# One phase in place of five at the end of each second-block layer: gates, MLA attention, head norms, branch products and output projection

## What is computed

```python
for i in range(DEPTH):                                  # DEPTH = 2
    u = rms_norm(h, norm_mix_g[i])
    z = u @ w_in[i]
    z_rwkv, z_mla, z_gdn, z_gate = split_cols_2(z, ...)
    o_a, v_first = rwkv7_branch(...)                    # ends in a per-head norm, a bonus and a gate
    o_b = mla_branch(...)                               # 8 heads, keys of 96, causal softmax
    o_c = gdn_branch(...)                               # ends in a per-head norm and a gate
    g_a, g_b, g_c = split(sigmoid(z_gate), 3)           # each 256 x 1024
    merged = g_a * (o_a @ w_br_rwkv[i]) + g_b * (o_b @ w_br_mla[i]) + g_c * (o_c @ w_br_gdn[i])
    h = h + merged @ w_out[i]
    u2 = rms_norm(h, norm_ffn_g[i])                     # then an FFN (layer 0) or a mixture of experts (layer 1)
```

## Time and profile before

| | us |
|---|---|
| median of 3 runs | 4079.12 (4063.91, 4079.12, 4082.13) |
| the profiled execution's own time | 4070.22 |
| its span | 4068.4 |
| TensorE busy | 3807.3 |
| VectorE, ScalarE, GpSimd busy | 727.7, 576.2, 155.3 |
| mean granted TensorE clock | 0.94 of 2.4 GHz |

### The profile page before, as it was taken

One profiled execution on the slowest core, in us unless ns is written; L12 is line 12 of the kernel. 1 busy time (PEld: TensorE's weight loads), 2 busy tenths in 40 slices (PEclk: granted clock), 3 DMA queues, 4 the chain that ended last, 5 costly groups with the idle time before them and its releaser, 6 DMA issues. The chain is left out here.

```text
span 4068.4 us, 45964 instructions
## 1 busy us (share of the span) xinstructions
PE 3807.3 (94%) x19340; PEld 2809.7 (69%) x19340; DVE 727.7 (18%) x1642; ACT 576.2 (14%) x1320; POOL 155.3 (4%) x107
## 2 busy tenths in 40 slices
PE   8998999999999988799999987969999999999999
PEld 6766677775676767546767676438787787787786
DVE  1023201004201354311013553120000000000001
ACT  1013201002201331101003312010010111010101
POOL 0000000000000021000101210010000000000000
PEclk9997999999999987699999976979999999999999
DMA  6321233333232400234324001418787787777863
GB/s 273 147 91 73 93 155 155 150 127 138 99 155 101 153 10 1 81 152 173 155 104 163 10 1 68 165 61 311 262 297 262 261 297 261 275 285 261 298 261 142
DMA packets 57336, 664.27 MB, mean 163 GB/s; under 512 B 7904, under 2 KB 8544, under 8 KB 11392
## 3 DMA queue, kind: packets, MB, share of 16 engines
q1 hardware_dynamic: 52272, 649.91, 42.1%
q10 hardware_dynamic: 4944, 12.65, 0.8%
HBM read 661.49 MB, written 1.05 MB: 163 GB/s over the span
## 5 line engine op out<-in xcount | busy, mean ns | idle before, releaser
L3237 PEld LDWEIGHTS psum<-arena,ring 128*128 128x128 f32 x7168 | 833.8, 191 | 111.7 <-issue 109.8
L3237 PE MATMUL psum<-arena,ring 128*128 128x128 f32 x7168 | 836.0, 274 | 8.2 <-DVE arena L3291 7.2
L613 PE MATMUL psum<-xT_norm,ring 128*128 128x256 f32 x3520 | 771.0, 380 | 0.0
L613 PEld LDWEIGHTS psum<-xT_norm,ring 128*128 128x128 f32 x3520 | 670.3, 191 | 112.7 <-issue 23.9
L3244 PE MATMUL psum<-ring,arena 128*128 128x512 f32 x896 | 420.3, 593 | 0.0
L624 PE MATMUL psum<-ring,arena 128*128 128x512 f32 x880 | 386.6, 592 | 0.0
L624 PEld LDWEIGHTS psum<-ring,arena 128*128 128x128 f32 x880 | 167.2, 190 | 187.0 <-issue 184.2
L3296 DVE TENSOR_TENSOR arena<-arena,psum 128x128 f32<-128x128 f32 x224 | 65.0, 290 | 1100.9 <-ACT arena L3275 1100.9
L672 DVE TENSOR_TENSOR arena<-arena,psum 128x256 f32<-128x256 f32 x110 | 46.4, 421 | 1061.9 <-ACT arena L653 1061.9
L3244 PEld LDWEIGHTS psum<-ring,arena 128*128 128x128 f32 x896 | 153.6, 191 | 110.9 <-issue 110.9
L3275 ACT ACTIVATE arena<-psum 128x128 f32<-128x128 f32 x224 | 62.5, 279 | 1140.0 <-PE psum L3237 1140.0
(11 more groups left out here) (496 smaller groups left out, 2899.9 us busy)
## 6 DMA issues: line engine op xcount, KB each, us to landing
ring<-in_moe_w SPq DMA_DIRECT2D x224, 1536.0 KB, 6.7
ring<-in_ffn_w SPq DMA_DIRECT2D x50, 3072.0 KB, 10.1
ring<-in_feat_w SPq DMA_DIRECT2D x12, 2048.0 KB, 8.5
ring<-in_merge_w SPq DMA_DIRECT2D x12, 2048.0 KB, 8.2
ring<-in_ffn_w SPq DMA_DIRECT2D x15, 1024.0 KB, 10.0
ring<-in_merge_w SPq DMA_DIRECT2D x12, 1024.0 KB, 7.2
ring<-in_ev_in_w SPq DMA_DIRECT2D x4, 2048.0 KB, 7.8
ring<-in_od_in_w SPq DMA_DIRECT2D x4, 2048.0 KB, 7.8
```

The costliest lines, as they stand in the source:

```text
L613: last = pe.matmul(prog.psum[:, t, m * S:(m + 1) * S], wm[:, k, t * P:(t + 1) * P], prog.xT[:, k, :], start=(k == 0), stop=(k == KT - 1))
L3237: last = pe.matmul(psum[:, s % 2, x * P:(x + 1) * P], m[:, x, i, :], xg[:, i, :], start=(i == 0), stop=(i == KT - 1))
```

## The change

Both layers' five phases become one, `join_branches`. What it does:

- The merge weights are packed anew into 11 pieces of 2 MB: six gate pieces, three branch pieces (both column halves of one branch), two projection pieces (four of the eight row blocks, all 1024 columns). The bytes are the same 22 MB per layer.
- Piece 0 is started on SP inside `chains`, once `r_made` has reached the first block's RWKV output; pieces 1 to 3 at the head of the new phase, the others as their ring places come free.
- TensorE's order is written out: the gate tiles stand between the steps of the attention and are kept in SBUF (12 tiles of 128 x 512); then the mixers' transposes, the other gates, the branch products, and the projection, whose first half of rows (`project(0)`) runs ahead of the transposes of the second half of the merged tile.
- The head norms run on VectorE, ScalarE and GpSimd in the same phase, between the attention's steps. Gate tiles use PSUM banks 5 to 7, branch products 4 and 5, scores 0 and 1, transposes 2 and 3, the projection 0 to 3.
- The three weight pieces of layer 0's feed-forward are started on SP after the branch products of MLA's second half.

```diff
 def chains(prog, layer, kept, o, merge_weights):
+        @ph.block.sync
+        def _(sp):
+            sp.wait_ge(r_made, R_MADE["y0"])
+            merge_weights.start(sp, 0)
...
-def finish_branches(prog, layer, kept, o, mem):
-def mla_attention(prog, kept, o):
-def merge(prog, weights, w_out, oT, merged):
+def join_branches(prog, layer, kept, o, weights, next_weights):
...
+        @ph.block.sync
+        def _(sp):
+            for i in (1, 2, 3):
+                weights.start(sp, i)
+            for n in range(5):
+                sp.wait_ge(gate_sum, TB * (n + 1))
+                weights.start(sp, 4 + n)
+            sp.wait_ge(gate_sum, TB * 6)
+            weights.start(sp, 9)
+            sp.wait_ge(branch_sum, 8)
+            weights.start(sp, 10)
+            if next_weights:
+                sp.wait_ge(branch_sum, 10)
+                for i in range(3):
+                    next_weights.start(sp, i)
...
+            def project(j):
+                weights.wait(pe, 9 + j)
+                for n, (b, c) in enumerate(columns):
...
+                    for k in range(4):
+                        if n == 0 and k % 2 == 0:
+                            pe.wait_ge(mT_copied[k // 2], j + 1)
+                        last = pe.matmul(psum[:, n, :], mT[:, 4 * j + k, b * P:(b + 1) * P], w[:, k, c * BANK:(c + 1) * BANK],
+                                         start=(j == 0 and k == 0), stop=(j == 1 and k == 3), skip_group_check=True)
...
+            score(0)
+            gate(0)
+            turn(0)
+            score(1)
+            gate(1)
+            values(0)
+            turn(1)
+            score(2)
+            gate(2)
+            values(1)
+            turn(2)
+            gate(3)
+            values(2)
+            gate(4)
+            gate(5)
+            turn_branch(0)
+            gate(6)
+            turn_branch(1)
+            gate(7)
+            turn_branch(2)
+            for n in range(8, 12):
+                gate(n)
+            for n in range(6):
+                branch(n)
+            branch(6)
+            branch(7)
+            turn_merged(0)
+            for n in range(8, 12):
+                branch(n)
+            project(0)
+            turn_merged(1)
+            project(1)
...
+            act.activation(squares[:, 1], by_head(g_y), ACT.Square).then_inc(head_squared, 1)
+            exponentials(0)
+            squash(0)
+            copy_turned(0)
+            act.wait_ge(centred, 1)
+            act.activation(squares[:, 0], by_head(r_y), ACT.Square).then_inc(head_squared, 1)
+            exponentials(1)
+            squash(1)
+            copy_turned(1)
+            exponentials(2)
+            squash(2)
+            copy_turned(2)
+            act.wait_ge(head_mean, 2)
+            act.activation(stat, stat, ACT.Sqrt).then_inc(head_rooted, 1)
+            squash(3)
...
             chains(prog, i, kept, o, mer)
-            mer.prefetch(0, 1, 2, 3)
-            finish_branches(prog, i, kept, o, mem)
-            mla_attention(prog, kept, o)
-            transposes(prog, [o[:, b, k * P:(k + 1) * P] for k in range(12) for b in range(TB)], oT.rearrange("p a b -> p (a b)"))
-            merge(prog, mer, out_w, oT, (merged, mem.at))
-            if i == 0:
-                ffn[4].prefetch(0, 1, 2)
-            add_projection(prog, out_w, merged, mT, mem.take(2, BANK))
+            join_branches(prog, i, kept, o, mer, ffn[4] if i == 0 else None)
```

More of the change, by code:

```diff
@@ L1601, with chains @@
 QUADS = 8
-def chains(prog, layer, kept, o):
+def chains(prog, layer, kept, o, merge_weights):
     r, g, psum = kept.r, kept.g, prog.psum
@@ L2924, in take, with __init__ @@
         return v.rearrange(f"p ({' '.join(names)}) -> p {' '.join(names)}", **kw)
-def finish_branches(prog, layer, kept, o, mem):
-    r, g = kept.r, kept.g
-    squares, bonus_v = mem.take(2, TB, NH8, HD), mem.take(TB, NH8, HD)
+class MergeWeights(Weights):
+    def __init__(self, prog, layer):
+        flat, pieces, at = prog.inp[f"merge_w{layer}"], [], 0
+        for place in (0, 1, 2, 3, 0, 1, 2, 3, 0, 1, 2):
+            n = P * KT * BANK
+            pieces.append((flat[at:at + n].rearrange("(p c) -> p c", p=P), place * KT * BANK))
+            at += n
+        super().__init__(prog, pieces)
@@ new lines, in join_branches @@
+def join_branches(prog, layer, kept, o, weights, next_weights):
+    r, g, psum, ident = kept.r, kept.g, prog.psum, prog.ident
+    early = Arena(prog, kept.free_at)
+    squares, bonus_v = early.take(2, TB, NH8, HD), early.take(TB, NH8, HD)
+    kept.load_rows(prog, layer, early)
+    oT = Arena(prog, kept.free_at).take(3, PAIRS, S)
+    t_sb, pT_sb = (Arena(prog, kept.kept_at).take(2, 2, 2 * BANK)[:, i] for i in range(2))
+    state_at = kept.qT_at - 2 * PAIRS * HD
+    least, total = Arena(prog, state_at).take(2, 3, 8)[:, 0], Arena(prog, state_at).take(2, 3, 8)[:, 1]
+    gates_a, gates_b = Arena(prog, kept.g_at).take(8, BANK), Arena(prog, kept.r_tok_at + TB * BANK).take(4, BANK)
+    gates = [gates_a[:, n] if n < 8 else gates_b[:, n - 8] for n in range(12)]
+    mT = Arena(prog, kept.qT_at).take(KT, S)
+    junk = Arena(prog, kept.kT_at).take(2, BANK)
@@ new lines, in join_branches @@
+    first = prog.const_at["zero"][0]
+    attended = ((0, 0, 4), (1, 0, 2), (1, 2, 2))
+    members = [[[x * 4 + at + j for j in range(n)] for x in range(2)] for b, at, n in attended]
+    keys = lambda i: (attended[i][0] + 1) * P
+    hidden_keys = lambda i: prog.consts[:, first + P - attended[i][0] * P:first + S]
+    probs_of = lambda i: t_sb[:, i % 2].rearrange("p (m n) -> p m n", n=keys(i))
+    value_bank, gate_bank = psum[:, 4, :], lambda n: psum[:, 5 + n % 3, :]
+    tiles = [(j, x, b) for j in range(2) for x in range(3) for b in range(TB)]
@@ new lines, in _ @@
+            exponentials(1)
[7 more added lines that the diff above has]
+            squash(3)
+            squash(4)
+            squash(5)
+            copy_branch(0)
+            squash(6)
+            copy_branch(1)
+            squash(7)
+            copy_branch(2)
+            for n in range(8, 12):
+                squash(n)
@@ new lines, in _ @@
+            for n in range(3):
+                copy_branch(n)
+            for n in range(8):
+                weigh(n)
+            copy_merged(0)
+            for n in range(8, 12):
+                weigh(n)
+            copy_merged(1)
+            for n, (b, c) in enumerate(columns):
+                dve.wait_ge(bank_full, n + 1)
+                at = prog.x[:, b, c * BANK:(c + 1) * BANK]
+                dve.tensor_tensor(at, psum[:, n, :], at, ALU.add).then_inc(tail.added, 1)
+            tail.on_vector(dve)
@@ L3434, in second_weights @@
     tok = chunk_weights(prog, prog.inp[f"tok_w{layer}"], TOK_CHUNKS, (4096, 14336))
-    flat, pieces, at = prog.inp[f"merge_w{layer}"], [], 0
-    for i in range(12):
-        n = P * (KT if i % 2 == 0 else 4) * BANK
-        pieces.append((flat[at:at + n].rearrange("(p c) -> p c", p=P), i % 4 * 4096))
-        at += n
-    return feat, tok, Weights(prog, pieces)
+    return feat, tok, MergeWeights(prog, layer)
 def build(nc, inp, tables, out):
```

341 lines of the change are left out of this document (231 added, 110 removed).

## The result

The changed kernel takes 4006.52 us (median of four executions, 4002.36 to 4018.45); the kernel before, run beside it on the same chip, 4077.36 (4063.91 to 4082.13). The ratio is 0.9836, 95% interval 0.9804 to 0.9869. The forecast was 4010, with 3993 to 4034 as its range.

What follows compares the result with a forecast made beforehand. TensorE, busy 94% of the span, was taken as the bound, with about 52 and 50 us of slack in the two layers. Phases of 176.4 us gain 33.9 and 31.0, together 64.9; from 4074.7 that gives 4010, range 3993 to 4034.

Steps and rivals of the forecast that it cites:

- The joined phase: Merged phase of each layer: 169.7 us of TensorE work plus entry, clock, waits and tail, 176.4 us in all.
- Margins: Hand-overs from VectorE and ScalarE in the attention: each group's probabilities ready 2 to 4 us before TensorE needs them.
- GpSimd's slowing: VectorE runs slower where GpSimd works on the same tiles; margins take most of it, 0.5 us added.
- Table loads: ScalarE's alternating exponentials and sigmoids: about nine loads a layer, 1.28 us each, no cost to TensorE if margins hold.
- The norms cost nothing, because gates cover them: Head norms in the merged phase: hidden behind gates; without that cover they would cost their 18 us again.
- Weights: Merge-weight loads, with piece 0 started 48 us ahead of the phase: all at zero; a late piece costs 8.8 to 18.6.
- other phases moving by more than a few us: Stated sign of a wrong prediction, beside a merged phase of over 190 us.
- A: Rival: attention hand-overs through VectorE and ScalarE still make TensorE wait, 6.3 + 6.5 us, about 4023; chance 0.10.
- B: Rival: clock falls between the gates, three falls a layer at about 2.8 us, 17 in all, 4027; chance 0.11.
- C: Rival: piece 0 lands late and gate 0 waits 5 to 15 us a layer, 4020 to 4040; chance 0.03.
- D: Rival: gates run at the low clock, 6.9 us more per tile, up to 165 us more, 4175; chance 0.02.
- The baseline: Starting point of the forecast: 4074.7 us, the middle of four executions from 4063.9 to 4082.1, 9 either way.

Runs made afterwards that it cites:

- e6: Changed kernel with five ScalarE copies of 128x1024 ahead of each group's exponentials, holding them back; 4040.90 us, 0.9914 of the kernel before.
- e3: Changed kernel with all attention steps first on TensorE, the first six gates after them, and ScalarE's first four sigmoids behind its square root; 4051.70 us.
- e1: Changed kernel with piece 0 of the merge weights started at the head of the joined phase instead of inside `chains`; 4021.01 us, 0.9876 of the kernel before.

## Why the prediction was right, and where not

- **The joined phase: right.** 176.4 us a layer were worked out, 175.0 and 174.6 measured. TensorE is busy for 171.8 and the other 3.2 are the entry (0.4), the copy ahead of `project(1)` (0.34 against 0.5) and the tail (2.51 against 2.5). The clock was up 6.0 us after the end of `chains` in layer 0 and 5.1 in layer 1, which is 5.6 and 4.7 after TensorE's first product (5.2 to 6.4 assumed); against full speed the scores and gate 0 lose some 3 us (3.75 for 16 records that were put at 1.7, 8.06 for a tile of 6.9), where the sum has 2.8. The transposes were put too high: eight in 0.87 us are 7.0 for 64, not 7.7.
- **Margins: right.** Foretold was group 0's probabilities at 9.5 us with gate 0's end at 12; they came at 9.8 and 11.8. For groups 1 and 2 about 2.5 us were foretold and 3.9 found, since `values` of the group before stands ahead of each `turn` and wasn't counted. The held exponentials show that the margins are real and that they are needed. GpSimd's slowing, 0.5 us in the sum, cost TensorE nothing.
- **Table loads: right.** Eight a layer (nine foretold), free, and no gain when half of them were taken out. "Nothing if the margins hold" was the right condition: in the run with held exponentials two loads of layer 0 showed, at 1.3 us each.
- **"The norms cost nothing, because gates cover them": right**, and without that cover they cost 18.2 and 18.8 us.
- **Weights: wrong.** "Piece 0 ... All at zero" failed for the recurrences. Its wait on SP held nothing up, but the landing itself cost TensorE 4.7 us in layer 0 and 3.2 in layer 1. The working looked only at SP's queue and due times, not at what else uses the DMA engines while the piece lands: TensorE's instructions. The prediction named other phases moving by more than a few us as a sign of being wrong, and this is such a move. The term should have been 8 us, and with it the same sum gives 57 for the two layers where the stretches show 60.3.
- **The rivals.** A: no wait at any `turn` or `values`; e6 makes one and pays for it. B: clock 1.00 from gate 1 on, with eight transposes or 16 records of 64 columns between the gates; but e3 and e6 show that such falls are real as soon as TensorE waits for some 3 us between the gates. The 7.8 us that e6 lost to the clock in layer 0 are near B's price of 8.4 a layer. C: no wait on a DMA; e1 makes one, 4.94 us, at the low end of the 5 to 15 given. D: no sign of it.
- **The baseline.** Forecast was a gain of 65. Three comparisons of the two kernels show medians 70.8, 69.5 and 59.1 us apart, the profiled stretches 60.3. The 8 us too many lie inside this spread, and no median would have shown them. That the median came within 4 us of the forecast is therefore partly luck: the recurrences lost 7.9 us that the sum didn't have, the phases gave 3.3 more than it had, and the rest is the spread of the executions.

What stays open: the records of the instruction transfers don't say which engine they are for, and no run moved them alone; that the gap waits for them rests on the times agreeing in every profile. That the clock falls earlier because of the gap rests on the same comparison. In layer 1 it holds only in part: with the early piece the fall comes at 8.4 to 11.3 us, and without it at 10.2 to 10.4 where a gap of 0.33 to 0.81 us is left, so there the longer gap is the steadier part of the loss.

## What to carry to other kernels

A phase that leaves TensorE idle and another that TensorE bounds can share their time if each hand-over to VectorE and ScalarE has a block of independent products as long as the hand-over; work out each margin from the timeline, because below zero it costs its length and the clock behind it. An early load isn't free because its queue is: the engines' instructions come by DMA too. Put it where the engines run few, long instructions, and measure the stretch that it lands in. A dense block of products ahead of a thin tail at the low clock can be worth more than its place in the order suggests.

## What was not expected of the hardware

- Starting a 2 MB load among 32 and 64-column products put an idle gap of 0.94 to 1.91 us on TensorE that only its own issue ends; the same load started some 20 to 40 us later, among fewer and longer products, put none in layer 0 and left one of 0.18 to 0.71 us in layer 1, where 0.33 and 0.81 us were seen with no load at all.
- A 16 KB instruction transfer landed about 1.2 us later beside that load, and TensorE's next product came 1.25 to 1.6 us after its landing in every such gap.
- In the 22 stretches with a gap of 0.33 us or more the clock fell 8.4 to 11.7 us behind the first RWKV output, in the six with none or 0.18 us at 14.0 to 15.1. This also holds for the kernel before, whose layer 1 (0.33 us, 10.2 us) ran the same recurrences 3.7 us longer than layer 0 (no gap, 14.0 us). With the early piece, a gap of 1.04 us made layer 0's stretch 4.7 us longer, one of 1.52 us layer 1's 3.2.
- With waits of 2.4 to 4.2 us between gates of 7 us (held exponentials, both layers) the clock went to 1.2 GHz each time, for 3.4 to 6.8 us. With eight transposes (0.87 us) or 16 records of 64 columns (1.7 us) in place of the wait it stayed at 2.4 GHz.
- One gate, 16 records of 512 columns, brings the clock from 1.2 up to 2.4 GHz in the middle of a thin stretch, and the 64 records of 64 columns behind it stay at 2.4 GHz to the end of `chains` (1.89 to 1.95 us for 16 instead of 3.6).
